# Modulation loads before the weights in the convolution stage, and the last four down-projection tiles by column halves

## What is computed

```python
# first block
h = rmsnorm(x, ffn_norm_w[l])
x = x + (jax.nn.silu(h @ w_gate[l]) * (h @ w_up[l])) @ w_down[l]       # 5632 hidden columns

# second block
c_act = jax.nn.silu(c)
mod = (c_act @ w_ada[l] + b_ada[l])[:, None, :]                       # w_ada: 2048 x 12288
sh1, sc1, g1, sh2, sc2, g2 = jnp.split(mod, 6, axis=-1)
h = rms_norm(x, norm_mix[l]) * (1.0 + sc1) + sh1
x = x + g1 * hybrid_mixer(h, ...)
h = rms_norm(x, norm_ffn[l]) * (1.0 + sc2) + sh2
x = x + g2 * conv_glu_ffn(h, ...)

def conv_glu_ffn(h, w_up, conv_w, conv_b, w_down):
    u = h @ w_up                                                      # 2 x 5632 columns
    u = sum(conv_w[j] * up[:, j:j + S] for j in range(CONV_WIDTH)) + conv_b
    val, gate = jnp.split(u, 2, axis=-1)
    return (jax.nn.silu(gate) * val) @ w_down
```

## Time and profile before

| | |
|---|---|
| median of 3 runs | 2617.44 us (2616.83 to 2619.86) |
| profiled execution | 2615.34 us |
| its span | 2613.6 us |
| TensorE busy | 97% of the span |
| VectorE, ScalarE busy | 63%, 44% |
| mean granted TensorE clock | 0.984 |
| modulation loads on the chain that ended last | 4% of the span |

### The profile page before, as it was taken

One profiled execution on the slowest core, in us unless ns is written; L12 is line 12 of the kernel. 1 busy time (PEld: TensorE's weight loads), 2 busy tenths in 40 slices (PEclk: granted clock), 3 DMA queues, 4 the chain that ended last, 5 costly groups with the idle time before them and its releaser, 6 DMA issues.

```text
span 2613.6 us, 41798 instructions
## 1 busy us (share of the span) xinstructions
PE 2526.0 (97%) x17370; PEld 2295.8 (88%) x17370; DVE 1634.7 (63%) x1924; ACT 1148.1 (44%) x1488; POOL 0.3 (0%) x5
## 2 busy tenths in 40 slices
PE   8999999999999999997999999999888999999997
PEld 8888778999999998886998999888788999997886
DVE  5566557767767757777586565566555665665545
ACT  5464344434343344444554334445333444444443
POOL 0000000000000000000000000000000000000000
PEclk9999999999999999998899999999899999999998
DMA  8454458687777767886565333554555555555552
GB/s 271 150 163 155 145 205 274 245 289 276 264 281 270 270 215 280 298 293 221 195 245 165 99 116 130 178 193 174 197 199 212 183 189 184 193 209 180 190 191 98
DMA packets 213836, 541.32 MB, mean 207 GB/s; under 512 B 9050, under 2 KB 14756, under 8 KB 201668
## 3 DMA queue, kind: packets, MB, share of 16 engines
q1 hardware_dynamic: 213700, 539.37, 59.1%
HBM read 534.06 MB, written 5.28 MB: 206 GB/s over the span
## 4 chain that ended last, share of the span: by engine, by line
PE 88%; DVE 6%; DMA 4%; issue 1%; ACT 1%; SPq 0%; DVEq 0%; ACTq 0%
PE ps L295 30%; PE ps L1598 18%; PE ps L468 16%; PE ps L1783 14%; DMA ada_w<-in_w_ada_dram 4%; DVE weights_lo L261 2%; DVE ada_acc L395 2%; PE ps L2267 1%; PE ps L2252 1%; PE ps L838 1%; PE ps L1731 1%; PE ps L862 1%; DVE conv_y L3079 1%; PE ps L2264 1%; PE ps L407 0%
## 5 line engine op out<-in xcount | busy, mean ns | idle before, releaser
L261 DVE TENSOR_TENSOR weights_lo<-raw_weights,weights_hi 128x1024 fp32r<-128x1024 f32 x794 | 966.8, 1224 | 780.5 <-ACT weights_hi L254 778.2
L254 ACT ACTIVATE weights_hi<-raw_weights 128x1024 fp32r<-128x1024 f32 x794 | 840.2, 1060 | 1302.4 <-PE ps L295 536.9
L395 DVE SCALAR_TENSOR_TENSOR ada_acc<-ada_w,col,ada_acc 128x1024 f32<-128x1024 f32 x180 | 230.3, 1279 | 85.3 <-DMA ada_w<-in_w_ada_dram 85.2
L295 PE MATMUL ps<-conv_x_hi,weights_hi 128*128 128x256 f32 x1280 | 210.2, 287 | 28.5 <-DVE weights_lo L261 28.5
L295 PEld LDWEIGHTS ps<-conv_x_hi,weights_hi 128*128 128x128 f32 x1280 | 178.7, 193 | 32.5 <-DVE weights_lo L261 31.6
L295 PE MATMUL ps<-conv_x_hi,weights_lo 128*128 128x256 f32 x1280 | 207.1, 284 | 0.0
L295 PE MATMUL ps<-conv_x_lo,weights_hi 128*128 128x256 f32 x1280 | 206.8, 284 | 0.0
L295 PE MATMUL ps<-glu_x_hi,weights_hi 128*128 128x256 f32 x1280 | 202.8, 280 | 0.0
L295 PE MATMUL ps<-glu_x_lo,weights_hi 128*128 128x256 f32 x1280 | 202.7, 280 | 0.0
L295 PE MATMUL ps<-glu_x_hi,weights_lo 128*128 128x256 f32 x1280 | 202.4, 279 | 0.0
L295 PEld LDWEIGHTS ps<-conv_x_hi,weights_lo 128*128 128x128 f32 x1280 | 177.8, 193 | 0.0
(11 more groups left out here) (453 smaller groups left out, 3711.4 us busy)
## 6 DMA issues: line engine op xcount, KB each, us to landing
raw_weights<-in_w_in_dram SPq DMA_DIRECT2D x101, 1024.0 KB, 5.8
ada_w<-in_w_ada_dram SPq DMA_DIRECT2D x96, 1024.0 KB, 7.1
raw_weights<-in_w_ffn_up_dram SPq DMA_DIRECT2D x88, 1024.0 KB, 4.9
raw_weights<-in_w_gate_dram SPq DMA_DIRECT2D x44, 1024.0 KB, 5.0
raw_weights<-in_w_up_dram SPq DMA_DIRECT2D x44, 1024.0 KB, 5.1
raw_weights<-in_w_down_dram SPq DMA_DIRECT2D x44, 1024.0 KB, 5.1
raw_weights<-in_w_ffn_down_dram SPq DMA_DIRECT2D x44, 1024.0 KB, 4.9
raw_weights<-in_w_out_dram SPq DMA_DIRECT2D x32, 1024.0 KB, 5.3
```

The source lines that it names most:

```text
L254: kit.nc.scalar.activation(kit.w_hi_t[:, n % SPLITS, :], raw, ACT.Copy).then_inc(kit.w_hi, 1)
L261: kit.nc.vector.tensor_tensor(kit.w_lo_t[:, n % SPLITS, :], raw, kit.w_hi_t[:, n % SPLITS, :].bitcast(F32), ALU.subtract).then_inc(kit.w_l ...
L295: ins = nc.tensor.matmul(out, lhsT=lhsT, rhs=rhs, start=start and m == 0, stop=(k == KT - 1 and m == 2), skip_group_check=True)
L395: step = nc.vector.scalar_tensor_tensor(acc, w, c, acc, ALU.mult, ALU.add)
```

## The change

In the convolution stage, a modulation load is issued ahead of the weight load of its place instead of behind it, the first two of a group come at once with their distance set by `GROUP`, and the products lie behind the splits of even steps: product s of the first group in step 2s + 6, of the second in step 2s + 44 (counted over the turns from 0). The sums lie behind unit 0 of the second half of turn 2 and behind unit 0 of turn 5; six turns are written out.

In both down-projections, the last four tiles are multiplied left half first, for all four tiles, and then right half. So the left sums are complete four units before the end. The additions and squares of the left half are put between the splits of the last units. In the first down-projection the 24 modulation loads and 48 products are spread over fewer tiles and end 12 units before the stage does. The next stage's first four loads wait for the splits of the last four units one by one (`split`), since raw buffers come free later. A scratch buffer (`m2_squares_2`) lies elsewhere.

```diff
@@ load, splits
-def load(kit, sp, l, i, src):
+def load(kit, sp, l, i, src, split=None):
     if l >= LOADS:
-        sp.wait_ge(kit.w_lo, 2 * (l - LOADS) + 2 + 16 * i)
+        sp.wait_ge(kit.w_lo, (2 * (l - LOADS) + 2 if split is None else split) + 16 * i)
@@ class Down
+    def order(self, p):
+        at = 2 * self.w_tiles - 8
+        return divmod(p, 2) if p < at else (self.w_tiles - 4 + (p - at) % 4, (p - at) // 4)
+    def tail(self):
+        return range(2 * self.w_tiles - 8, 2 * self.w_tiles)
@@ Down.sync
-            return max(0, 2 * loads * (k - 5) // (2 * w_tiles - 3))
+            return min(loads, max(0, 2 * loads * (k - 5) // (2 * w_tiles - 15)))
...
-            self.head_next(sp, first // 2 + w_tiles)
+            self.head_next(sp, first // 2 + w_tiles, first + 2 * w_tiles - 3)
@@ Down.scalar
+        for p in self.tail():
+            if not self.last or p + AHEAD < 2 * w_tiles:
+                split_hi(kit, act, first + p + AHEAD, 0, self.ahead(p, 0))
+            if p == self.tail()[4]:
+                bring_root(kit)
+            if p in self.tail()[5:7]:
+                self.squares(act, p - self.tail()[5])
+        self.squares(act, 2)
+        self.squares(act, 3)
@@ Down.vector
-        if steps:
-            self.ada.product(dve, self.lead + steps // 16 - 1, 0, 15, self.accs[-1])
+        for p in self.tail():
+            unit(p, 0)
+            if p in self.tail()[4:6]:
+                self.add(dve, p - self.tail()[4])
+        self.add(dve, 2)
+        self.add(dve, 3)
@@ class ConvGlu
-    BEGUN = 5
+    BEGUN, GROUP = 6, 38
-        return i // 2 - 1 if isinstance(i, int) and i in (2, 4) else None
+        at = [(2, 1), (5, 0)]
+        return at.index((i, j)) if isinstance(i, int) and (i, j) in at else None
@@ ConvGlu.sync
             for m in range(8):
+                for g in range(2):
+                    a, odd = divmod(8 * i + m - self.GROUP // 2 * g, 2) if isinstance(i, int) else (0, 1)
+                    if not odd and 0 <= a < 8:
+                        if a == g == 0:
+                            sp.wait_ge(kit.weights_used, first)
+                        self.ada.load(sp, lead + g, 0, a)
                 if m < 4 or not (isinstance(i, int) and i == self.turns - 1):
                     col = (0, F2 + UN)[m // 4] + UN * i
                     load(kit, sp, first // 2 + 4 + m, i, block_src(self.w, m % 4, col))
-                if isinstance(i, int) and i < 4 and m % 2:
-                    if i == 0 and m == 1:
-                        sp.wait_ge(kit.weights_used, first)
-                    self.ada.load(sp, lead + i // 2, 0, 4 * (i % 2) + m // 2)
@@ ConvGlu.vector
-                    if isinstance(i, int) and i < 4 and u % 2:
-                        self.ada.product(dve, lead + i // 2, 0, 8 * (i % 2) + 4 * j + u // 2)
+                    for g in range(2):
+                        s, odd = divmod(16 * i + 8 * j + u - 6 - self.GROUP * g, 2) if isinstance(i, int) else (0, 1)
+                        if not odd and 0 <= s < 16:
+                            self.ada.product(dve, lead + g, 0, s)
```

More of the change, by code:

```diff
@@ L1605, in tensor, with body @@
+        def body(k, i):
+            for half in range(2):
+                unit(2 * k + half, k, half, i)
         self.in_turns(pe, body)
+        for p in self.tail():
+            unit(p, *self.order(p), 0)
     def ada_sums(self, pe):
@@ L1634, in lo_tile, with ahead @@
                                     ).then_inc(kit.a_lo, 1)
-    def over(self, k, half, past):
-        return self.last and k + past >= self.w_tiles - 2 + (1 - half)
+    def ahead(self, p, i):
+        return None if not isinstance(i, int) else self.source(p + AHEAD)
     def scalar(self, act):
@@ L1673, in vector @@
         steps = 16 * len(self.accs)
-        def body(k, i, past):
-            for half in range(2):
-                if not self.over(k, half, past):
-                    split_lo(kit, dve, first + 2 * k + half + AHEAD, i)
-                if steps:
-                    u = 2 * k + half - 3
-                    units = 2 * w_tiles - 3
-                    for s in range(max(0, steps * (u - 1) // units), max(0, steps * u // units)):
-                        self.ada.product(dve, self.lead + s // 16, 0, s % 16, self.accs[s // 16])
-            if k + past + 4 < w_tiles:
-                self.lo_tile(dve, k + 4, i)
@@ L1686, in vector, with unit @@
[L1686 to L1703 removed]
+        def unit(p, i):
+            if not self.last or p + AHEAD < 2 * w_tiles:
+                split_lo(kit, dve, first + p + AHEAD, i, self.ahead(p, i))
+            if steps:
+                units = 2 * w_tiles - 15
+                due = lambda u: min(steps, max(0, steps * u // units))
+                for s in range(due(p - 4), due(p - 3)):
+                    self.ada.product(dve, self.lead + s // 16, 0, s % 16, self.accs[s // 16])
@@ new lines, in body, with add @@
+        def body(k, i):
+            for p in (2 * k, 2 * k + 1):
+                unit(p, i)
+            self.lo_tile(dve, k + 4, i)
+        self.in_turns(dve, body)
+        for p in self.tail():
+            unit(p, 0)
[3 more added lines that the diff above has]
+        self.add(dve, 3)
+    def add(self, dve, n):
+        kit, nc = self.kit, self.kit.nc
+        half, t = self.ends[n]
+        cols = slice(half * D // 2, (half + 1) * D // 2)
+        if t == 0:
+            dve.wait_ge(kit.down_sums, self.out + half + 1)
+        else:
+            dve.wait_ge(kit.weights_used, self.first + 2 * self.w_tiles - 4 + 4 * half)
+        sums, x = self.sums_of(half, t), kit.x[:, t, cols]
+        if self.gate is not None:
+            kit.dve(nc.vector.tensor_tensor(sums, sums, self.gate[:, cols], ALU.mult))
+        nc.vector.tensor_tensor(x, sums, x, ALU.add).then_inc(kit.x_added, 1)
+        if self.weighted:
+            dve.wait_ge(kit.loaded, self.loaded)
+            dve.wait_ge(kit.x_added, self.added + n + 1)
+            nc.vector.tensor_tensor(self.weighted[0][:, t, cols], x, self.final_w[:, cols], ALU.mult
+                                    ).then_inc(self.s_y, 1)
```

148 lines of the change are left out of this document (68 added, 80 removed).

## The result

| | before | after |
|---|---|---|
| median of 4 runs, us | 2617.36 (2616.83 to 2619.86) | 2535.85 (2534.04 to 2539.32) |
| profiled execution, span | 2615.34, 2613.6 | 2534.04, 2532.1 |
| ratio, 95% interval | | 0.9688 (0.9672 to 0.9705) |

What follows compares the result with a forecast made beforehand. The convolution stage was taken as bound by the landing of modulation loads asked for too late. Savings of 55.7 (convolution), 5.8 and 2.0 us (down-projection tails) sum to 63.5, giving a median of 2553.9 us, range 2546 to 2566.

Steps and rivals of the forecast that it cites:

- turns 0 and 1: Convolution stage: turn 0 falls from 60.79 to 54.8 us, saving 6.0; turn 1 runs clean at 45.2 us.
- products away from their loads: Convolution stage: products six steps (17.0 us) behind their load's issue, against 7.0 us landing, so none waits; 55.7 us saved.
- the pace behind the row sums: Convolution stage: turns clean at 45.23 us, the two row sums only adding 1.98 us each; turns 2 and 5 at 47.2.
- Weights behind modulation: Convolution stage: weight loads 2 to 5 us late at step 16 against some 6 us cushion; priced at nothing, bounds 0 and 10.
- Tails: Behind the down-projections: first gains 5.8 us (bounds 3.4 and 7.3), second 2.0 us (bounds 1.5 and 2.5).
- Rival C: Tails of both down-projections give nothing, or the lower clock behind the gap lasts longer; 2561.7 us, chance 0.08.
- Clock pricing: Convolution turns 1 to 3: lower clock priced at half the throttled time makes 45.0 us, against 49.1 by turn times.
- D: Convolution stage: the stall only halves, a product still meeting its load in flight; 2582 us, chance 0.03.
- E: Convolution stage: weight loads behind modulation waits reach TensorE late at 14 loads, slower than before; 2641 us at 24 us landing, chance 0.02.

Runs made afterwards that it cites:

- weights_first: The changed kernel with the weight load ahead of the modulation load again, the products keeping their new places; 2536.25 us.
- no_sums: The changed kernel without the two groups' row sums in the convolution stage, so its result lacks their modulation; 2545.53 us.
- conv_alone: The kernel before with the new convolution stage and the old down-projections, scratch buffer moved as in the change; 2544.63 us, ratio 0.9712 to before.
- conv_again: The kernel before with the new convolution stage alone, run a second time beside the changed kernel; 2548.69 us, ratio 0.9750 to before.
- glu_wide: The changed kernel plus two 512-column float32 products of constants behind unit 8 of Glu's turns 1, 3, 5, 7 and 9; 2542.52 us.

## Why the prediction was right or wrong

**Direction, bound, and turns 0 and 1: right.** The stage was bound by a landing asked for too late. With the products moved, the stalls and the lower clock are gone, and turn 0 gave 6.0 us as summed. `weights_first` shows that the order of the loads is not what did it, which leaves "products away from their loads".

**The step that failed: the pace behind the row sums.** I took 45.23 us for a clean turn from turns 5 on of the kernel before and held it for a property of TensorE at clock 1.00, and I put turns 2 and 5 at 47.2 us. Behind the first row sums a turn takes 43.52, and turns 2 and 5 took 46.2 and 45.2. From there to the stage's end that makes the whole 14.8 us that the stage gave beyond 55.7. The row sums were in my sum only as a cost of 1.98 us each; in `no_sums`, without them, every turn takes the 45.23 us that I had forecast. What sets the pace behind a group of sums stays open: the same program took the fast one at its first sums in `conv_alone` and not in `conv_again`. So part of the gain beyond the forecast is luck; at 45.23 us throughout the time would have been some 2551 us (2535.9 + 14.8), inside my range. Nothing in the profile of before showed the other pace as possible, since its gated network and its convolution both ran at 45.2; but my range held no term for "the same matmuls may run at another pace", and that is why the time fell out of it. The rest of the miss is 1.7 us of the second mixer, 0.7 ahead of it and 0.6 of the first tail.

**Weights behind modulation: right on the cost, and the cushion is the reason given.** ScalarE waited five times and at most 3.7 us, where I had 2 to 5 us late against a cushion of 6, at one place; TensorE did not idle. The landings are those of a load behind a megabyte: the modulation loads took 7.0 us when they were issued second and 4.9 when first, the weights 4.9 and 7.2. The Trainium skill ("DMA: Bandwidth & Descriptors", "Queues, rings and completion order") says that each DMA engine takes descriptors in ring order, and these landings agree with it. The effect on the time was none.

**Tails: right.** 6.4 us against 5.8 behind the first down-projection, since the last split came 1.1 instead of 1.5 us late, and 2.0 against 2.0 behind the second. The lower clock did not stay as I expected: granted clock below full lasts 10.2 us in place of 17.1 from the gap on. The time that this saves lies in the second mixer, where it can't be told from the variation. Rival C is out. What I did not see is that in the old stage this gain is lost again.

**Clock pricing.** The Trainium skill's way ("TensorE: Matmul & The Clock Gate", Terms) gave 45.0 us for turns 1 to 3, mine 49.1. Mine held the row sum of turn 2, so 47.1 for the stalls alone. `conv_again` ran turns 1 to 3 at the old pace, in 45.23 + 46.94 + 45.23 = 137.4 us; the stalls were 184.8 - 137.4 = 47.4 us. The Trainium skill's way is 2.4 us short here.

**Rivals D and E** had no sign: no product waited, and no landing came near 22 us.

## What to carry over

A work step put one step behind its own load turns every small disturbance of the landing into idle time and a lower clock: move the use away from the issue first, and care about the order of issue later. Test the parts of a change in each other's company as well as alone, since a stage that is bound by a landing can eat what another stage gains. And the same matmuls at the same clock do not have one pace only: where a change moves what stands between them (here sums and waits), leave room for the other pace in the range, and read a result turn by turn before giving it to the edit.

## What the runs showed of the hardware

- TensorE has two steady paces at granted clock 1.00: 113.3 and 117.8 ns for a 256-column matmul with its weight load (43.52 and 45.23 us for 384). A pair of 512-column float32 products can switch it to the fast one (13 of 20 times without a gap, once in 14 behind a wait), and float32 products of one column ended it both times in `glu_wide`. A wait alone can switch it too: the fast pace began nine times behind a wait of 0.4 to 2.7 us in the kernels with the old stage, and lasted up to the next one. What decides is open, so 10 to 15 us of this kernel's time rest on something that is not controlled.
- Packets of the instruction queue come over the same DMA engines as the data: 16 KB in 128 matmuls on average, 1.0 us of one engine. The 20 loads of 1 MB that had one 2.6 to 5.9 us behind their issue took 8.3 to 8.6 us instead of some 7.1.
- Of two 1 MB loads issued together, the second lands in 7.0 to 7.2 us by the medians and the first in 4.9 to 5.1, whichever is which.
